# Scan turns moved to the 17th unit of their own group and joined with the former group's sum of squares, and one unread product ahead of the output projection's loop

## The reference, cut to what matters

```python
z, xbc, dt = _split(h @ w_in, [SSM_D_INNER, SSM_CONV_DIM, SSM_N_HEADS])
xbc = jax.nn.silu(causal_dwconv(xbc, conv_w, conv_b))
...
y = ssd_chunked(xs, dt, a, bm, cm)          # scan over 2 chunks of 128 positions
y = y + d_skip * xs
y = y * jax.nn.silu(z)
yg = yg * lax.rsqrt(jnp.mean(yg * yg, axis=-1, keepdims=True) + EPS)   # per group
y = yg * norm_w
return y @ w_out
```

## Time and profile before

| | |
|---|---|
| median of 3 runs | 2575.72 us (2574.93 to 2576.14) |
| profiled execution | 2575.84 us, span 2574.2 us |
| instructions | 46083 |
| PE, DVE, ACT, POOL busy | 2568.0, 1791.6, 1415.9, 220.7 us |
| DMA | 481.59 MB, mean 187 GB/s |

### The profile page before, as it was taken

The page is one execution under the profiler, slowest core; times in us unless marked ns, Lnnn a source line. Parts: engine busy times, 40 slices in busy tenths (PEclk is TensorE's granted clock), DMA queues, the critical chain, the costliest instruction groups (busy, mean ns, idle before and its releaser), DMA issues.

```text
span 2574.2 us, 46083 instructions
## 1 busy us (share of the span) xinstructions
PE 2568.0 (100%) x15223; PEld 2253.1 (88%) x15223; DVE 1791.6 (70%) x2592; ACT 1415.9 (55%) x2182; POOL 220.7 (9%) x197
## 2 busy tenths in 40 slices
PE   9999999999999999999999999999999999999999
PEld 8888888888888888888888888888888888888888
DVE  8787877875677777775555686777777777775444
ACT  6767667754455555554444465665555555554333
POOL 0211222122100000000111000102200000000000
PEclk9999999999999999999999999999999999999999
DMA  6655665655565555556666575334555556556665
GB/s 213 236 197 190 200 197 196 203 178 184 179 196 188 190 187 187 193 188 187 189 188 194 193 232 201 117 98 140 187 189 188 188 186 194 188 187 186 189 190 169
DMA packets 139483, 481.59 MB, mean 187 GB/s; under 512 B 17329, under 2 KB 19441, under 8 KB 138384
## 3 DMA queue, kind: packets, MB, share of 16 engines
q1 hardware_dynamic: 136448, 467.20, 57.1%
q0 software_dynamic: 2368, 12.68, 1.4%
q10 hardware_dynamic: 592, 0.71, 0.1%
HBM read 478.28 MB, written 2.16 MB: 187 GB/s over the span
## 4 chain that ended last, share of the span: by engine, by line
PE 91%; DVE 4%; ACT 2%; issue 2%; ACTq 0%; DVEq 0%; POOL 0%; POOLq 0%
PE ps L838 48%; PE ps L837 25%; PE pq L838 5%; PE po L838 3%; PE pq L837 3%; PE po L837 1%; DVE w_lo L1257 1%; PE po L1140 1%; DVE cv L1365 1%; ACT w_hi L441 1%; ACT wcum L536 0%; PE pq L1126 0%; PE ps L897 0%; PE pq L855 0%; PE pq L856 0%
## 5 line engine op out<-in xcount | busy, mean ns | idle before, releaser
L1257 DVE TENSOR_TENSOR w_lo<-raw,w_hi 128x1024 fp32r<-128x1024 f32 (+1 forms) x896 | 1094.5, 1224 | 613.6 <-ACT w_hi L441 612.5
L441 ACT ACTIVATE w_hi<-raw 128x1024 fp32r<-128x1024 f32 (+1 forms) x896 | 933.2, 1043 | 803.1 <-PE ps L838 698.5
L838 PE MATMUL ps<-xn,w_hi 128*128 128x512 f32 x3904 | 1358.8, 392 | 0.0
L837 PE MATMUL ps<-xn,w_lo 128*128 128x256 f32 x3904 | 1098.2, 281 | 0.4 <-DVE gpad L1266 0.2
L838 PEld LDWEIGHTS ps<-xn,w_hi 128*128 128x128 f32 x3904 | 730.4, 187 | 159.3
L837 PEld LDWEIGHTS ps<-xn,w_lo 128*128 128x128 f32 x3904 | 737.7, 189 | 4.6 <-DVE w_lo L1257 1.8
L838 PE MATMUL ps<-hid,w_hi 128*128 128x512 f32 x1408 | 488.2, 391 | 0.0
L837 PE MATMUL ps<-hid,w_lo 128*128 128x256 f32 x1408 | 394.2, 280 | 0.0
L838 PEld LDWEIGHTS ps<-hid,w_hi 128*128 128x128 f32 x1408 | 263.3, 187 | 57.7
L837 PEld LDWEIGHTS ps<-hid,w_lo 128*128 128x128 f32 x1408 | 266.1, 189 | 0.0
L838 PE MATMUL pq<-xn,w_hi 128*128 128x512 f32 x528 | 184.4, 391 | 0.0
(11 more groups left out here) (297 smaller groups left out, 2446.6 us busy)
## 6 DMA issues: line engine op xcount, KB each, us to landing
raw<-w_gu SPq DMA_DIRECT2D x352, 512.0 KB, 3.8
raw<-w_ssm_in SPq DMA_DIRECT2D x158, 512.0 KB, 3.8
raw<-w_down SPq DMA_DIRECT2D x128, 448.0 KB, 3.8
raw<-w_nsa_in SPq DMA_DIRECT2D x82, 512.0 KB, 4.2
raw<-w_ssm_out SPq DMA_DIRECT2D x64, 512.0 KB, 3.6
raw<-w_down SPq DMA_DIRECT2D x64, 512.0 KB, 4.0
raw<-w_nsa_out SPq DMA_DIRECT2D x32, 512.0 KB, 3.7
wcum<-cum_scratch POOLq DMA_DIRECT2D x8, 1024.0 KB, 7.9
```

The costliest lines, as they stand in the source:

```text
L441: act.activation(w_hi[:, slot, 0:n * P], raw[:, slot, 0:n * P], ACT.Copy).then_inc(unit_rounded, 1)
L837: pe.matmul(acc[:, n:2 * n], w_lo[:, slot, cols], x[:, kb, 0:n], start=(kb == 0), stop=False, skip_group_check=True)
L838: mm = pe.matmul(acc[:, 0:2 * n], w_hi[:, slot, cols], x[:, kb, 0:2 * n], start=False, stop=(kb == n_blocks - 1), skip_group_check=True)
L1257: TT(w_lo[:, slot, 0:n * P], raw[:, slot, 0:n * P], w_hi[:, slot, 0:n * P].bitcast(F32), ALU.subtract).then_inc(unit_split, 1)
```

## The change

In PE's order the turn of group g moves from behind unit 0 of body g + 1 to behind unit 16 of body g, and the sum of squares of group g - 1 from unit 14 to unit 16, directly before it; the sum goes to bank 5 instead of bank 4 (but for the last group). ACT's copy `sbt` and DVE's `xdt` and `xw` move with the turn to step 17, the root to step 17, the norm to step 18, the rounding to step 19 and the rest to step 0 of the body after (two bodies after its group's). The last group's turn thus lies in the in-projection. Ahead of the loop over the out-projection's other bodies stands one product that nobody reads.

```diff
--- before.py
+++ after.py
@@ -541,8 +541,9 @@
                 act.activation(xdt[:].rearrange("p c n -> p (c n)"), yz[:].rearrange("p a t -> p (a t)"), ACT.Square).then_inc(ysq_ready, 1)
 
             def scan_std(g):
+                total = ps[4] if is_body(g, GROUPS - 1) else ps[5]
                 act.wait_ge(gss_done, g + 1)
-                act.activation(grs[:], ps[4][:, 0:T], ACT.Sqrt, scale=1.0 / (XT_G * P), bias=eps[:, 0:1]).then_inc(gstd_ready, 1)
+                act.activation(grs[:], total[:, 0:T], ACT.Sqrt, scale=1.0 / (XT_G * P), bias=eps[:, 0:1]).then_inc(gstd_ready, 1)
 
             def scan_round(g):
                 act.wait_ge(yn_ready, g + 1)
@@ -564,17 +565,16 @@
                             conv_silu(g, k - 1)
                     elif k >= 7:
                         z_silu(g, k - 7)
-                    if scan:
-                        for at, stage in SCAN_ACT:
-                            if at == v:
-                                stage(g - 1)
-                    else:
+                    if not scan:
                         dt_part(v)
+                    for at, back, stage in SCAN_ACT:
+                        if at == v and (scan or not back):
+                            stage(g - back)
                 z_silu(g, 3)
 
             DECAY_ENDS = 5
-            SCAN_ACT = ((1, scan_sbt), (3, scan_ecum), (3, lambda g: scan_decay(g, 0)), (4, lambda g: scan_decay(g, 1)),
-                        (11, scan_square), (14, scan_std), (16, scan_round))
+            SCAN_ACT = ((3, 1, scan_ecum), (3, 1, lambda g: scan_decay(g, 0)), (4, 1, lambda g: scan_decay(g, 1)),
+                        (11, 1, scan_square), (17, 0, scan_sbt), (17, 1, scan_std), (19, 1, scan_round))
             p = ph["ssm"]
             ssm_body(0, (p.sizes * 3)[RING:], scan=False)
             loop(act, 1, p.n - 1, lambda g: ssm_body(g, (p.sizes * 3)[RING:]))
@@ -582,7 +582,7 @@
             ssm_body(p.n - 1, unit_sizes[end:end + p.body])
             def last_scan_step(v):
 
-                for at, stage in ((1, scan_sbt), (2, scan_ecum), (2, lambda g: scan_decay(g, 0)), (2, lambda g: scan_decay(g, 1)),
+                for at, stage in ((2, scan_ecum), (2, lambda g: scan_decay(g, 0)), (2, lambda g: scan_decay(g, 1)),
                                   (2, lambda g: scan_decay(g, 2)), (6, scan_square), (8, scan_std), (9, scan_round)):
                     if at == v:
                         stage(GROUPS - 1)
@@ -944,7 +944,6 @@
                 pe.wait_ge(conv_act, 6 * g + 6)
                 pe.wait_ge(tk_ready, 1)
                 pe.wait_ge(xdt_ready, g)
-                pe.wait_ge(gstd_ready, g)
                 pe.wait_ge(yz_step, 2 * g)
                 for c in range(2):
                     cut = slice(c * L, (c + 1) * L)
@@ -967,39 +966,46 @@
                 mm.then_inc(y_done, 1)
 
             def scan_sumsq(g):
+                total = ps[4] if is_body(g, GROUPS - 1) else ps[5]
                 pe.wait_ge(sq_summed, g + 1)
-                pe.matmul(ps[4][:, 0:T], ones[:], xdt[:, 0, 0:T], start=True, stop=True).then_inc(gss_done, 1)
+                if not is_body(g, GROUPS - 1):
+                    pe.wait_ge(tile_out, ph["ssm"].tile0 + 7 + (g + 1) * ph["ssm"].per_body)
+                pe.matmul(total[:, 0:T], ones[:], xdt[:, 0, 0:T], start=True, stop=True).then_inc(gss_done, 1)
 
             p = ph["ssm"]
-            SCAN_PE = ((0, scan_turn), (9, scan_y), (14, scan_sumsq))
+            SCAN_PE = ((9, 1, scan_y), (16, 1, scan_sumsq), (16, 0, scan_turn))
 
             def ssm_body(g, scan=True):
                 for v in range(0 if scan else 4, p.body):
+                    if scan and v == 2:
+                        pe.wait_ge(gstd_ready, g - 1)
                     gemm_unit(p, g, v, xn)
-                    if scan:
-                        for at, stage in SCAN_PE:
-                            if at == v:
-                                stage(g - 1)
-                    elif v == 15:
+                    for at, back, stage in SCAN_PE:
+                        if at == v and (scan or not back):
+                            stage(g - back)
+                    if not scan and v == 15:
                         turn_dt()
 
             ssm_body(0, scan=False)
             loop(pe, 1, p.n, ssm_body)
             p = ph["ssm_out"]
             for v in range(p.body):
-                if v == 6:
-                    pe.wait_ge(y_ready, GROUPS - 1)
+                if v == 0:
+                    pe.wait_ge(y_ready, GROUPS - 2)
+                if v == 3:
+                    pe.wait_ge(gstd_ready, GROUPS - 1)
                 if v == 12:
                     pe.wait_ge(y_ready, GROUPS)
                 gemm_unit(p, 0, v, y_ssm)
-                for at, stage in ((0, scan_turn), (6, scan_y), (8, scan_sumsq)):
+                for at, stage in ((6, scan_y), (8, scan_sumsq)):
                     if at == v:
                         stage(GROUPS - 1)
+            def spacer(at, x):
+
+                pe.matmul(ps[at][:, 0:T], ones[:], x, start=True, stop=True)
+
+            spacer(3, xdt[:, 0, 0:T])
             gemm(p, y_ssm, first=1)
-
-            def spacer(at, x):
-
-                pe.matmul(ps[at][:, 0:T], ones[:], x, start=True, stop=True)
 
             def ffn(l, p_gu, p_down):
                 gemm_first(1 + 2 * l, p_gu)
@@ -1409,7 +1415,7 @@
                 dve.wait_ge(y_rounded, g + 1)
                 TT(y_ssm[:, bass.ds(g * XT_G, XT_G), T:2 * T], yz[:], y_ssm[:, bass.ds(g * XT_G, XT_G), 0:T].bitcast(F32), ALU.subtract).then_inc(y_ready, 1)
 
-            SCAN_DVE = ((1, scan_xdt), (5, scan_w), (10, scan_yz), (15, scan_norm), (17, scan_rest))
+            SCAN_DVE = ((0, 2, scan_rest), (5, 1, scan_w), (10, 1, scan_yz), (17, 0, scan_xdt), (18, 1, scan_norm))
             p = ph["ssm"]
 
             def ssm_body(g, nxt, scan=True):
@@ -1422,10 +1428,9 @@
                         conv_tap_of(g, k - 1, 1)
                     if v % 2 and k < 6:
                         conv_pad(p, g, k)
-                    if scan:
-                        for at, stage in SCAN_DVE:
-                            if at == v:
-                                stage(g - 1)
+                    for at, back, stage in SCAN_DVE:
+                        if at == v and (not back or scan and (back == 1 or not is_body(g, 1))):
+                            stage(g - back)
                     if taps:
                         conv_tap_of(g, k - 1, 0)
                     if not scan and v == 1:
@@ -1444,7 +1449,9 @@
             ssm_body(p.n - 1, unit_sizes[end:end + p.body])
             def last_scan_step(v):
 
-                for at, stage in ((1, scan_xdt), (6, scan_yz), (8, scan_norm), (9, scan_rest)):
+                if v == 0:
+                    scan_rest(GROUPS - 2)
+                for at, stage in ((6, scan_yz), (8, scan_norm), (9, scan_rest)):
                     if at == v:
                         stage(GROUPS - 1)
```

More of the change, by code:

```diff
@@ L994, in _ @@
                 gemm_unit(p, 0, v, y_ssm)
-                for at, stage in ((0, scan_turn), (6, scan_y), (8, scan_sumsq)):
+                for at, stage in ((6, scan_y), (8, scan_sumsq)):
                     if at == v:
                         stage(GROUPS - 1)
-            gemm(p, y_ssm, first=1)
             def spacer(at, x):
                 pe.matmul(ps[at][:, 0:T], ones[:], x, start=True, stop=True)
+            spacer(3, xdt[:, 0, 0:T])
+            gemm(p, y_ssm, first=1)
             def ffn(l, p_gu, p_down):
```

## The result

| | before | after |
|---|---|---|
| median | 2575.72 us (5 runs) | 2586.80 us (5 runs, 2585.52 to 2588.77) |
| profiled execution, span | 2575.84, 2574.2 us | 2587.73, 2586.0 us |

The ratio is 1.0046, 95% interval 1.0035 to 1.0057: slower by 11 us.

A forecast was written before the change was run, and what follows sets the result against it. PE was taken as the bound, busy 2568.0 of 2574.2 us. Terms -1.5 - 2.4 + 1.9 + 12.7 + 3.4 + 0.2 = +14.3 gave about 2590.0 us against the median; range 2576.5 to 2597.0, the forecast's own 2583 to 2596.

The forecast's parts named there:

- Fewer stops: Loop's sums of squares joined to turns: four waits for POOL and a slow stretch saved, -1.5 us.
- First turn: Moved to unit 16 of body 0, it waits for ACT's copy of the step sizes: +1.9 us, once.
- The late remainder: In the loop, rest at step 0 delays POOL's work and the silu: PE waits 2.1 us per body, 12.7 in six.
- B: The end of unit 19 of a loop body, from which the prediction counts its times in us.
- 3.5 for taps and masks together: In the loop, DVE's three taps and POOL's two masks take turns, 3.5 us together, ahead of the first silu.
- The cover: Margin in the loop between the last weighting's end on DVE and the y that needs it: 1.13 us.
- The last group: Its y, after unit 6 of the projection, waits behind rest, POOL's product and masks: +3.4 us.
- The unread product: Behind unit 12 of the projection's first body, it restores the fast pace: 2.8 saved, 0.43 cost, net -2.4 us.
- Rival 1: The loop keeps its cover: y never waits if step 3's silu slips under 1.13 us; 2577.3 us, chance 0.20.
- Rival 3: PE's clock falls after the longest wait, one or two units at half pace: about 2594 us, chance 0.10.

The follow-up runs named there:

- e1: The kernel after without the unread product, everything else as it is: 2587.62 us, ratio to before 1.0044.
- e3: The kernel after with POOL's two masks ahead of its wait for the late rest and ahead of its product: 2575.65 us, ratio to before 0.9997.
- e2: The kernel before with the unread product alone added ahead of the out-projection's loop: 2574.07 us, ratio to before 0.9994.
- e11: The kernel after with masks first, first turn one unit later and rest ahead of unit 0's split, unread product kept: 2571.42 us, ratio to before 0.9983.
- e4: The kernel after with the first group's turns one unit later: 2585.97 us, ratio to before 1.0035.

## Why the prediction was right, and where it was off

The forecast was 2590.0; the kernel takes 2586.8, inside the forecast's own range, and by the mechanism that was named. That the sums lie so close (14.3 and 12.1) is in part luck: the waits were put 4.7 us too high, and the slow pairs, 2.5 us, stood in no term.

- *Fewer stops*: right. The four waits for POOL went, seven stops cost 1.96 each, and no new wait appeared in the bank or the root.
- *First turn*: the wait was right to 0.1 us. That a stop in which PE waits can also leave the slow pace (+0.7 here, nothing in e1's profile) was not foreseen: the stops of the kernel before, from which the pace was judged, wait 0.3 us at the most, and one of eight sums left it.
- *The late remainder*: each link to the split of step 2 is within 0.15 us of the count: rest's end B + 9.4 (9.3), POOL's product to B + 12.3 (12.3), split to B + 13.4 (13.4). The term that was mis-sized is "3.5 for taps and masks together": it took 3.1, because the third tap met no mask. The silu came at 5.4 us behind unit 3 instead of 5.9. The cover was right: 13.99 us from silu to y before, 12.91 when PE waits, so 1.08 (1.13 forecast). Hence 1.2 to 1.6 us a body instead of 2.1: 8.6 instead of 12.7 us.
- *The last group*: the masks ended at B + 14.9 instead of 15.5, so the y waited 2.7 and its stop cost 2.8 us more instead of 3.4 (the prediction's own terms, 22.7 - 19.4, give 3.3). That the masks come onto its chain, which they were not on before, was right; e3 takes them off and the wait goes.
- *The unread product*: the reading failed that a plain product "restores the pace" which was lost at a fixed place. It does end a slow stretch (e2, e11), but whether there is one differs from execution to execution, and the profile of the kernel after had none there. The -2.9 came about, in this profile by luck.
- *Rival 1* had the right deciding point, the silu of the body, and the wrong side of it: it slipped 2.75 us, where the point was 1.13. *Rival 3* did not show in the profile of the kernel after and did in that of e4; the mean clock of 0.999 in two of the five runs of the kernel after suggests that it came there too.

## What to carry to other kernels

When a step moves, look at what it releases on a second engine and what that then runs beside: here the moved instruction itself cost next to nothing, and the two masks queued behind its wait cost 11 us. Work that doesn't depend on a wait belongs ahead of it in its engine's order. On an engine that is 99% busy a wait is dearer than its length, since the stream may come out of it at a slower pace; remove the last 0.2 us too.

## What the runs showed of the hardware

- **Two paces of one stream at granted clock 1.00.** A pair takes 346.7 or 353.3 ns, from one stop to the next. Over the loop's stops in the twelve profiles (turns, y, sums, joint stops): of 139 in which PE waited for nothing, 3 were followed by the slow pace; of 55 in which it waited 0.03 us or more (by the excess of the stop), 26 were. What makes the difference inside PE no row shows, and no run tried it.
- **DVE instructions with two SBUF inputs and POOL instructions that read SBUF take turns, and either side can lose**: two masks take 2.32 us in a quiet stretch, 3.12 to 4.10 beside splits and taps, a tap 0.48 or 1.30, a split 1.22 or 2.58.
- **The granted clock can fall after a single wait of 2.7 us, and need not**: in one of three profiles, where it fell 0.9 us after the wait had ended, not in it; by the mean granted clock probably in ten of fifteen runs.
